# Columns in place of rows, a late root, and four sections of modulation tiles on GpSimd

## The reference

```python
h = rms_norm(x, norm_g)              # x * rsqrt(mean(x*x) + eps) * gain, per token
proj = h @ w_in                      # 2048 x 12368: attention, recurrence and gate projections
...
h = x + merged @ w_out               # merged: gated sum of the attention and the hgrn2 branch
# second block, with a context of 256 tokens and a condition vector c
mod = silu(c) @ ada_w + ada_b        # 2048 x 12288: shift, scale, gate, twice (6 sections)
hx = rmsnorm(x, norm1_g) * (1 + scale) + shift
hc = rmsnorm(ctx, norm1_g) * (1 + scale_c) + shift_c       # from silu(c_ctx) @ ada_w
x = x + gate1 * (merge_groups(neighbourhood_attention, fourier_mix, hyena_mix) @ w_out)
x = x + gate2 * conv_gated_mlp(rmsnorm(x, norm2_g) * (1 + scale2) + shift2)
out = rmsnorm(x, final_norm_g)
```

## Time and profile before

| | us |
|---|---|
| three runs, median | 2409.99 (2407.58 to 2412.49) |
| the profiled execution | 2409.62 |
| its span, first to last instruction | 2407.6 |
| PE busy | 2304.9 (96%) |
| DVE busy | 1281.3 (53%) |
| ACT busy | 1040.4 (43%) |
| POOL busy | 6.2 |
| mean granted clock of TensorE | 0.986 of 2.4 GHz |
| DMA | 469.61 MB, mean 195 GB/s |

### The profile page before, as it was taken

How to read it: one execution, slowest core, us unless ns; L and a number is a source line. 1 busy time by engine, 2 the same in 40 slices (tenths; PEclk the granted TensorE clock), 3 DMA queues, 4 the chain that set the end, 5 groups by cost and what they waited for, 6 DMA issues and landing times.

```text
span 2407.6 us, 39058 instructions
## 1 busy us (share of the span) xinstructions
PE 2304.9 (96%) x17166; PEld 2080.3 (86%) x17166; DVE 1281.3 (53%) x1601; ACT 1040.4 (43%) x1439; POOL 6.2 (0%) x9
## 2 busy tenths in 40 slices
PE   6999999889999998899999999989999999999997
PEld 4989988678889998888878899989999999998885
DVE  3456546656545455346445455655444555555564
ACT  5444334324345444434343354544433444444453
POOL 1000000000000000000000000000000000000000
PEclk9999999999999999999999999999999999999998
DMA  6756556446646877577754453446676555555562
GB/s 203 239 205 210 181 174 208 158 158 210 210 143 227 279 241 253 183 236 268 241 174 149 131 162 107 151 147 244 236 246 221 191 184 184 191 180 195 194 195 97
DMA packets 342934, 469.61 MB, mean 195 GB/s; under 512 B 20713, under 2 KB 316828, under 8 KB 329117
## 3 DMA queue, kind: packets, MB, share of 16 engines
q1 hardware_dynamic: 342765, 467.12, 58.3%
HBM read 465.00 MB, written 2.10 MB: 194 GB/s over the span
## 4 chain that ended last, share of the span: by engine, by line
PE 65%; DVE 3%; DMA 2%; ACT 2%; issue 1%; ACTq 0%; DVEq 0%
PE ps L1626 14%; PE ps L1628 14%; PE ps L1627 14%; PE ps L1639 3%; PE ps L1640 3%; PE ps L1638 3%; PE ps L1662 2%; DMA raw<-w_out_dram 1%; DVE wlo L1028 1%; ACT whi L494 1%; DMA raw<-w_in_dram 1%; PE ps L1648 1%; PE ps L1649 1%; PE ps L1650 1%; PE ps L1875 1%
## 5 line engine op out<-in xcount | busy, mean ns | idle before, releaser
L1028 DVE TENSOR_TENSOR wlo<-raw,whi 128x1024 fp32r<-128x1024 f32 (+1 forms) x668 | 813.3, 1222 | 1057.4 <-ACT whi L494 1054.1
L494 ACT ACTIVATE whi<-raw 128x1024 fp32r<-128x1024 f32 (+1 forms) x668 | 700.7, 1055 | 1209.1 <-PE ps L1628 655.4
L1626 PE MATMUL ps<-phi,whi 128*128 128x256 f32 (+1 forms) x3872 | 1130.6, 292 | 11.3 <-DVE plo L1391 6.7
L1627 PE MATMUL ps<-plo,whi 128*128 128x256 f32 (+1 forms) x3872 | 1097.0, 283 | 0.0
L1628 PE MATMUL ps<-phi,wlo 128*128 128x256 f32 (+1 forms) x3872 | 1096.4, 283 | 0.0
L1626 PEld LDWEIGHTS ps<-phi,whi 128*128 128x128 f32 x3872 | 736.5, 190 | 70.7 <-issue 49.8
L1627 PEld LDWEIGHTS ps<-plo,whi 128*128 128x128 f32 x3872 | 734.6, 190 | 8.6 <-issue 7.1
L1628 PEld LDWEIGHTS ps<-phi,wlo 128*128 128x128 f32 x3872 | 736.9, 190 | 0.3
L1638 PE MATMUL ps<-whi,dhi 128*128 128x512 f32 x352 | 136.9, 389 | 0.0
L1640 PE MATMUL ps<-wlo,dhi 128*128 128x512 f32 x352 | 136.9, 389 | 0.0
L1639 PE MATMUL ps<-whi,dlo 128*128 128x512 f32 x352 | 136.9, 389 | 0.0
(11 more groups left out here) (327 smaller groups left out, 2169.9 us busy)
## 6 DMA issues: line engine op xcount, KB each, us to landing
raw<-w_in_dram SPq DMA_DIRECT2D x152, 1024.0 KB, 5.5
raw<-ada_w_dram SPq DMA_DIRECT2D x96, 1024.0 KB, 9.6
raw<-ffn_w_up_dram SPq DMA_DIRECT2D x88, 1024.0 KB, 5.1
raw<-ffn_w_down_dram SPq DMA_DIRECT2D x44, 1024.0 KB, 5.3
raw<-w_out_dram SPq DMA_DIRECT2D x32, 1024.0 KB, 5.4
raw<-w_branch_dram SPq DMA_DIRECT2D x16, 1024.0 KB, 7.9
arena<-x_dram SPq DMA_DIRECT2D x2, 2048.0 KB, 10.2
arena<-ctx_dram SPq DMA_DIRECT2D x1, 2048.0 KB, 14.9
```

Of the source, the lines that this page charges most:

```text
L494: nc.scalar.activation(whi[c % 4][:, 0:w], src, ACT.Copy).then_inc(S("split_hi"), 1)
L1028: v.tensor_tensor(wlo[c % 4][:, 0:w], src, whi[c % 4][:, 0:w].bitcast(F32), ALU.subtract).then_inc(S("split_lo"), 1)
L1626: mm(o, wh[:, k], xk, start=st, stop=False)
L1627: mm(o, wh[:, k], yk, start=False, stop=False)
```

## The change

1. **Columns.** The host gives x, the context and all small vectors as columns (`xT`, `ctxT`, `vecT`: the reshape and transpose only). The loads of rows, the transposes of x, x rows and context, and the row norms in tokens are gone. The residual's x is loaded straight into `x1T`.
2. **Late root.** For the four units of FB, the planes `r_hi` and `r_lo` are x times gain without the norm. PE sums the squares by four products for each quarter of x, ACT and DVE make 1 / root, and DVE multiplies the result of FB by it when it leaves PSUM (`forget`). In slots 2 to 18 DVE and ACT make the normed planes for QB and all that follow.
3. **Norms.** In F and OB, DVE adds the squares of the units (`sums`); PE has one product per norm (`mean`). The context's norm is made alike in the last slots of E and the first of F.
4. **GpSimd.** Tiles 0 to 31 stay on PE. Tiles 32 to 95 are multiplied by their number per partition and added up by POOL, in halves of 1024 columns (`ada_half`), in units GB, E, F, G, H, IH, three of IQ, OA and OB, and the first 16 of L. Five closings follow: PE adds the sum over the partitions with a matrix of ones (four matmuls, in `slot`). The ring entry of such a tile is released by POOL (`ada_acc`).

On PE, at slot 171 in GB, chunk 171 of before ends with a modulation tile; then chunk 172 begins (`ps2`).

PE waits for no squares there any more. The core of the diff:

```diff
-for _u in range(48):
-    ADA_AT[_u, 1] = _u
+for _n in range(32):
+    ADA_AT[_n, 1] = _n
+for _n in range(16):
+    ADA_AT[U0["GB"] + _n, 1] = 32 + _n
...
+CLOSE = [(0, 15, SH1, 61), (16, 31, SC1, C0[31] + 1), (32, 47, G1, START["F"] - 1), (48, 63, SH2, START["IH"] - 1),
+         (64, 69, SC2, START["IF"] - 1), (70, 79, SC2, START["OB"] + 11), (80, 95, G2, START["L"] + 63)]
-            RELEASE.append(("ada_mm", ADA_AT[_u, _h] + 1))
+            RELEASE.append(("ada_mm", _n + 1) if _n < ADA_PE else ("ada_acc", 2 * (_n - ADA_PE) + 2))
...
 # SP
-            sp.dma_start(xin[:, 1:3, :], A["x"].rearrange("b (t p) n -> p (b t) n", p=128)).then_inc(S("x_in"), 16)
-            sp.dma_start(xin[0:META, 0, :], A["meta_tokens"]).then_inc(S("x_in"), 16)
+            sp.dma_start(cols[:, :], A["vecT"]).then_inc(S("vec_in"), 16)
+            for g in range(4):
+                sp.dma_start(xT[:, 4 * g:4 * g + 4, :], A["xT"][:, 4 * g:4 * g + 4, :]).then_inc(S(f"x_in{g}"), 16)
...
 # POOL
+            def ada_half(n, half):
+                ...
+                if half == 0:
+                    pool.wait_ge(S(f"loaded{e % RING}"), 16 * LOADED[e])
+                if n == CLOSE[k][0]:
+                    pool.wait_ge(S("mm"), C0[UNIT_OF_TILE[n]])
+                    ...
+                else:
+                    pool.wait_ge(S("ada_acc"), 2 * (n - ADA_PE) - 1 + half)
+                w = slice(1024 * half, 1024 * half + 1024)
+                by = cst[:, n % 16, 0:1]
+                if n == CLOSE[k][0]:
+                    t = nc.gpsimd.tensor_scalar(acc[k][:, w], raw[e % RING][:, w], by, None, ALU.mult)
+                else:
+                    x = raw[e % RING][:, w]
+                    nc.gpsimd.tensor_scalar(x, x, by, None, ALU.mult).then_inc(S("ada_scaled"), 1)
+                    ...
+                    t = nc.gpsimd.tensor_tensor(acc[k][:, w], x, acc[k][:, w], ALU.add)
+                t.then_inc(S("ada_acc"), 1)
...
 # ACT
-            planes(0, lambda kt: cols[:, V_NG + kt:V_NG + kt + 1], None, T)
-            for c in range(4):
-                hi(c)
+            def raw_planes(g):
+                act.wait_ge(S(f"x_in{g}"), 16)
+                for kt in range(4 * g, 4 * g + 4):
+                    nc.scalar.activation(r_hi[:, kt, :], xT[:, kt, :], ACT.Copy, scale=cols[:, V_NG + kt:V_NG + kt + 1]).then_inc(S("raw_hi"), 1)
+                nc.scalar.activation(sqs[:, 4 * g:4 * g + 4, :], xT[:, 4 * g:4 * g + 4, :], ACT.Square).then_inc(S("x_sq"), 1)
+            for g in range(3):
+                raw_planes(g)
+            hi(0)
+            hi(1)
+            raw_planes(3)
...
 # DVE
+            def forget(u, i):
+                ...
+                    m = v.tensor_tensor(f_flat[:, T * (2 * i + h):T * (2 * i + h) + T], ps[2 * p + h][:, 0:T], inv0, ALU.mult)
+            def sums(s, k, first, sqx, total):
+                ...
+                    v.tensor_tensor(total, total, sqx[:, i % 2, :], ALU.add).then_inc(S("sq_add"), 1)
...
 # PE
-                if q % 2 == 1 and (u, q // 2) in ADA_AT:
-                    ada_tile(ADA_AT[u, q // 2])
+                if q == 1 and (u, 1) in ADA_AT and ADA_AT[u, 1] < ADA_PE:
+                    ada_tile(ADA_AT[u, 1])
+                k = CLOSE_AT.get(c)
+                if k is not None and k >= 2:
+                    pe.wait_ge(S("ada_acc"), 2 * (CLOSE[k][1] - ADA_PE) + 2)
+                    ...
+                    for j in range(4):
+                        l = mm(ps[7][32 * j:32 * j + 32, :], ones32[:, :], acc[k][:, 512 * j:512 * j + 512], start=True, stop=True)
+                    l.then_inc(S("ada_sum"), 1)
+            def row_squares(g):
+                pe.wait_ge(S("x_sq"), g + 1)
+                for kt in range(4 * g, 4 * g + 4):
+                    l = mm(ps[4][:, 0:T], mean1[:, :], sqs[:, kt, :], start=kt == 0, stop=kt == KT - 1)
-                    for h in range(2):
-                        l = mm(ps[6][:, 0:256], mean1[:, :], sqx[:, i % 2, 256 * h:256 * h + 256], start=i + h == 0, stop=i + h == 8)
+            def mean(k, total):
+                pe.wait_ge(S("sum_T"), k + 2)
+                mm(ps[6][:, 0:256], mean1[:, :], total[:, 0:256], start=True, stop=True).then_inc(S("res_mean"), 1)
```

More of the change, by code:

```diff
@@ L467, in _ @@
             nc.gpsimd.memset(Kt, 0.0).then_inc(S("hg_zero"), 1)
+            for n in range(ADA_PE, 96):
+                for half in range(2):
+                    ada_half(n, half)
         @block.scalar
@@ L832, in context, with squares @@
-                    nc.scalar.activation(c_hi[:, kt, :], ptmp[:, kt % 2, 0:256], ACT.Copy).then_inc(S("pl_hi"), 1)
-            def squares(s, k, first, sqx):
+                    nc.scalar.activation(c_hi[:, kt, :], ctxT[:, kt, :], ACT.Identity, bias=modC[:, kt:kt + 1]).then_inc(S("pl_hi"), 1)
+            def squares(s, k, first, sqx, total):
                 u, q = CHUNK[s]
@@ L1156, in slot @@
                         glu(u, i)
-                n = ADA_AT.get((u - 1, 1))
-                if q == 1 and n is not None and n % 16 == 15:
-                    modulation(n // 16)
+                k = CLOSE_AT.get(c - 2)
+                if k is not None and CLOSE[k][2] != G2:
+                    modulation(k)
             l0, l1 = cols[:, V_LB:V_LB + 8], cols[:, V_LB + 8:V_LB + 16]
@@ L1354, in attention @@
                     v.tensor_tensor(y_lo[:, k:k + 4, :], rx(y, 4), y_hi[:, k:k + 4, :].bitcast(F32), ALU.subtract).then_inc(S("y_lo_set"), 1)
-            for t in range(3):
-                n = META if t == 0 else 128
-                normed(t, xin[0:n, t, :], xin[0:n, t, :], n)
-            planes(0, T)
-            for c in range(4):
-                lo(c)
+            dve.wait_ge(S("vec_in"), 16)
+            for g in range(3):
+                raw_planes(g)
+            lo(0)
+            lo(1)
+            raw_planes(3)
+            lo(2)
+            lo(3)
             for c in slots("FB", "GB"):
+                if c == S_PL + 1:
+                    dve.wait_ge(S("pl_tmp"), 1)
                 slot(c)
+                first_planes(c)
                 recurrence(c)
@@ L1382, in inverse @@
                 chain(v.reciprocal(dst, src))
+            def sums(s, k, first, sqx, total):
+                u, q = CHUNK[s]
+                i = u - U0[first] - 1
+                if q == 0 and 1 <= i < 8:
+                    dve.wait_ge(S("res_sq"), 8 * k + i + 1)
+                    v.tensor_tensor(total, total, sqx[:, i % 2, :], ALU.add).then_inc(S("sq_add"), 1)
+                    own("sq_add")
+                    if i == 7:
+                        v.tensor_tensor(total[:, 0:256], total[:, 0:256], total[:, 256:512], ALU.add).then_inc(S("sum_T"), 1)
             def stream_tmp(kt, gain, inv):
@@ L1529, in _ @@
                 context(c)
+                sums(c, 0, "F", sqx_f, sum_f)
                 if c == START["G"] + 2:
@@ L1540, in _ @@
                 neighbourhood(c)
+                sums(c, 1, "OB", sqx_o, sum_o)
+            sums(START["L"], 1, "OB", sqx_o, sum_o)
             inverse(1, inv2, root2)
@@ L2051, in _ @@
                 slot(c)
[L2052 removed]
                 context(c)
[L2054 removed]
+                if c == START["G"] + 1:
+                    mean(0, sum_f)
                 filters(c)
@@ L2183 @@
     given = {n: _np.ascontiguousarray(inputs[n]) for n in _INS}
+    given.update(columns(inputs))
     given.update(constants())
```

421 lines of the change are left out of this document (221 added, 200 removed).

## The result

| | before | after |
|---|---|---|
| median of five runs, us | 2409.6 (2407.0 to 2412.49) | 2418.39 (2417.51 to 2423.68) |
| span of the profiled execution | 2407.6 | 2416.6 |
| PE busy | 2304.9 (96%) | 2241.6 (93%) |
| DVE busy | 1281.3 (53%) | 1482.5 (61%) |
| POOL busy | 6.2 | 769.7 (32%) |

The ratio after / before is 1.0044, interval 1.0029 to 1.006. The forecast of 2325 was wrong, and so was its sign: the kernel is a little slower, by 0.3 to 0.6%. PE is busy for 63.3 us less than before and idle for 72.3 us more (175.0 against 102.7).

The account below looks back on a forecast made before the run. The prediction took PE, busy 96% of the span, as the bound. 2407.6 - 19 (start) - 59.5 (tiles) - 36 (F, norms) + 25 (GpSimd) + 5 (loads) = 2323, plus 2.0 outside the span: 2325 us; range 2283 to 2395.

Parts of the forecast that it names:

- What GpSimd costs: GpSimd's tiles meeting DVE's work in GB to G and early L: a third of the full cost, +25 us.
- the tile: One modulation tile on GpSimd: scale 0.9, add 1.8, waits 0.4, so 3.1 us a half, 6.2 to 7 a tile.
- the meeting: GpSimd's tiles beside DVE's two-input splits: 65 to 70 us if they exclude each other, 0 if not; a third taken.
- R2: GpSimd and DVE exclude each other, GB to G and early L run at their sum: 65 to 70 us; chance 0.22.
- R3: GpSimd becomes the bound in 48 units, kernel slower than before, from a tile of 8.0 us on; chance 0.10.
- The start: First weight matmul at 16 to 18 us instead of 37.68: -21, less 2 for the last squares' products.
- R4: The head start is lost, weights late in FB: gain at the start 10, time 2336 us; chance 0.04.
- The 64 tiles: PE loses 69 us of tiles, gains 5.5 of closings, 4 given back for the attention chain: -59.5 us.
- F and the norms: In F and the second block's norms, waits for squares, products, transposes and half-clock stretches go: -36 us.
- The loads: Loads at 274 GB/s where E had 253 and F 197, with x and context besides: +5 us.

Follow-up runs that it names:

- e8: The changed kernel with the 118 scales on GpSimd replaced by a memset of the same 1024 columns: 2356.22 us, ratio 0.9781.
- e10: The changed kernel, DVE's product one slot earlier, scale and add of 59 GpSimd tiles replaced by six memsets per half: 2312.78 us, ratio 0.9595.
- e11: The changed kernel, DVE's product one slot earlier, GpSimd's scale as a tensor_tensor with the number spread over the columns: 2412.84 us, ratio 1.0016.
- e14: The changed kernel in its own order, scale and add of 59 GpSimd tiles replaced by one copy of 8 columns: 2299.9 us, ratio 0.9545.
- e9: The changed kernel, DVE's product one slot earlier, scale and add of 59 GpSimd tiles replaced by three memsets per half: 2288.05 us, ratio 0.9492.
- e5: The changed kernel, DVE's product one slot earlier, scale and add of 59 GpSimd tiles replaced by one copy of 8 columns: 2286.24 us, ratio 0.9488.
- e12: The changed kernel, DVE's product one slot earlier, tiles 40 to 63 on PE behind the fourth chunk, 32 to 39 and 64 to 95 on DVE: 2320.84 us.
- e13: e12 with the tiles of E, F, G and H on PE behind the second chunk, all but the first of F: 2308.77 us, ratio 0.9586.
- e1: The changed kernel with all modulation tiles on PE in the units of the kernel before, none on GpSimd: 2380.56 us, ratio 0.9882.

## Why the prediction was wrong, step by step

**The step that failed is "What GpSimd costs": +25, measured +118.5.** With the rest as predicted, 2325 - 25 + 118.5 = 2418.5. It failed in two sizes. First the tile: scale 0.9 and add 1.8 were taken near the memset, the low bound; alone they are 2.85 and 2.39 us, a tile 10.5, beyond the upper bound of 9.0. A memset reads nothing and said little on operations that read; that the add of two inputs is the shorter of the two was not in the sum's logic either. Second the meeting, of which the prediction took a third because nothing in its rows decided. With a tile of 7.0 whose scale does not even read (e8) the cost is 2356.2 - 2299.9 = 56.3, more than twice the 25 and near the 65 to 70 of R2. The remaining 62 us come with the scale, by its length and by its own meetings, and no run parts the two exactly. Length is the lesser: 11.5 us without reading cost 26.5 (e10), and a tile of 8.6 alone, inside the prediction's bounds, costs 126.6 when its scale holds DVE's splits back (e11).

By stage, after less e14: GB 7.7, E 26.3, F 24.3, G 20.8, H 11.9, IH 5.3, OB 3.7, L 18.9. It is not an even price per unit, as R2 and R3 had it (GB loses 1.0 a unit, E 3.3, G 5.2): it is large where DVE carries chains that PE waits for, the context's and the residual's norm. That the chains are the reason is read from the waits for the two means; no run took them out.

**R3 was the right rival**, by its place, its rule (decides from a tile of 8.0) and its sign; its price was not: at 10.5 its formula gives 2295 + 94 + 3.5 x 48 - 25 = 2532. A unit need not be as long as tile plus DVE: in GB the 93.2 busy us of POOL and the 63.0 of DVE fit into 103.0, and later splits run beside a scale's last part.

The Trainium skill, "SBUF — State Buffer", section "Who interferes with whom", had the rule that decided, and the forecast gave it a third. e9 and e10 agree with its half on instructions that only write (split 1225 ns), and the pieces in F, held to the end of an add, with its whole-instruction lock. For the scale the lock is not for the whole instruction: it waited at its start as the rule has it (4.88 us in place of 2.85), but the splits at 732.52 ran within it in their own 2.36 us.

**The start** was right in its first step, 16.87, and wrong after it: 19 had been booked as kept; where IB begins, 2.6 are left without GpSimd's work (e14) and 14.5 with the product one slot earlier (e5). The work of slots 2 to 18 had no term in the sum at all. Weights in FB were not late (it takes 55.1 us, 55.0 before), so R4 named the right place for the wrong reason.

**The 64 tiles** gave what was said: L is 18.1 us shorter in e14, for 16 tiles at 1.08 = 17.3. **F and the norms**: F is 31.5 us shorter in e14, of which 8 tiles are 8.6, so 22.9, and OB 2.1: 25 of 36, inside the bounds. **The loads** cost next to nothing: in e5 PE is idle for no microsecond of GB at 262 GB/s, and for 2.4 of E at 299. **What no term had**: from IB to the start of GB e14 gains 29.7 us, nine tiles are 9.7 of them. The rest goes with shorter waits in the recurrence (16.4 us of PE's waits before at the one line, 10.9 now) and the clock behind them; tiles of units 0 to 31 moved from behind the fourth to behind the second chunk, the edit that gave 12 us between e12 and e13. e1 has all of the change but these tiles' new places, and gains 1.4 there: so the gain comes with the tiles' move. What of it is the earlier place in the unit, beside the smaller number, is argued from e13 and not shown.

So without GpSimd's work the changed kernel stands at 2299.9, and the prediction's sum for it was 2300. That is an accident: the start was booked 16 too high and the norms 11, what lies between IB and GB 20 too low, the loads cost 5 less, and the tiles gave 2 more.

## What to carry to other kernels

Before work is moved to GpSimd, price the operation by one of its own kind, reading as much as it does, and count a two-input operation of DVE beside it as time in which one of the two may stand still; a memset is evidence for neither. Then ask where DVE carries a chain that PE waits for: idle DVE is what counts, and in those stages the tile is cheaper on the busy PE (1.08 us) than on an idle GpSimd. Where an operation stands in an in-order loop between engines, write the loop down and sum it against the pace of the bound, and check when a shared buffer comes free as well as what the work costs.

## What the runs showed of the hardware

- GpSimd, 1024 float32 columns by 128 partitions: memset 0.96 us, scale with a number per partition 2.85 alone, the same as a tensor_tensor with the number spread over the columns 1.90 alone (2.57 in the mean, e11), add of two tensors 2.39 alone.
- GpSimd's tensor_scalar waits for two-input operations of DVE that are under way at its start (4.88 against 2.85), and most that begin later run beside it (88 of 124 splits in under 1.26 us). GpSimd's tensor_tensor holds them to its end: DVE's piece of 0.48 takes 2.62, and a split that begins inside an add 2.60 in the mean. Changing one form for the other took 115 us from POOL's scale and put 151 on DVE's split, and the kernel was 5 us slower (2412.8 against 2407.8).
- Memsets on GpSimd leave DVE's split as it is (1225 ns with 5.7 us of them per tile, e9; 1223 with 11.5, e10).
- An operation of two SBUF inputs and a pointer on DVE (1024 columns, 1.28 us) does scale and add at once, in a quarter of the time of GpSimd's two alone (5.24).
